# Gating two evictions behind until the fourteenth chunk, and other products in front of the third and fourth ffn_up steps

## What is computed

```
def conv_ffn(h, w_up, conv_w, conv_b, w_down, rows, cols):
    z = (h @ w_up).reshape(b, rows, cols, 2 * D_FF)
    z = lax.conv_general_dilated(z, conv_w[:, :, None, :], window_strides=(1, 1), padding='SAME', ...,
                                 feature_group_count=2 * D_FF)
    z = z.reshape(b, l, 2 * D_FF) + conv_b
    return (jax.nn.silu(z[..., :D_FF]) * z[..., D_FF:]) @ w_down
```

## Time and profile before

| | |
|---|---|
| median of 3 runs | 726.49 us (726.19 to 726.83) |
| profiled execution | 727.04 us in all, span 725.1 us |
| TensorE busy | 711.3 us (98%), mean granted clock 0.998 |
| VectorE, GpSimd, ScalarE busy | 497.7, 390.5, 364.4 us |
| chunks (ffn_up 1 to ffn_down 10) | 265.05 to about 447 us |

### The profile page before, as it was taken

One profiled execution on the slowest core, in us unless ns is written; L12 is line 12 of the kernel. 1 busy time (PEld: TensorE's weight loads), 2 busy tenths in 40 slices (PEclk: granted clock), 3 DMA queues, 4 the chain that ended last, 5 costly groups with the idle time before them and its releaser, 6 DMA issues.

```text
span 725.1 us, 14262 instructions
## 1 busy us (share of the span) xinstructions
PE 711.3 (98%) x5866; PEld 689.2 (95%) x5866; DVE 497.7 (69%) x919; ACT 364.4 (50%) x482; POOL 390.5 (54%) x225
## 2 busy tenths in 40 slices
PE   6899999999999999999999999999999999999998
PEld 3798889999999999999999999999999999999998
DVE  4886897569616569987777774557956666566563
ACT  6689235245434676555555556445563534334331
POOL 0767553547557958698888888766786000000000
PEclk9999999999999999999999999999999999999999
DMA  8994878336634565365555554433435655654511
GB/s 360 421 413 175 348 296 308 151 117 234 233 117 147 202 252 179 129 233 195 213 175 180 213 189 174 160 132 118 164 129 181 226 197 170 214 200 168 215 59 59
DMA packets 21234, 145.85 MB, mean 201 GB/s; under 512 B 2481, under 2 KB 3249, under 8 KB 3890
## 3 DMA queue, kind: packets, MB, share of 16 engines
q1 hardware_dynamic: 21024, 144.87, 55.1%
q10 hardware_dynamic: 146, 0.07, 0.0%
HBM read 143.88 MB, written 1.05 MB: 200 GB/s over the span
## 4 chain that ended last, share of the span: by engine, by line
PE 97%; DVE 1%; ACT 1%; issue 1%; DMA 0%; ACTq 0%; DVEq 0%
PE bank L1514 25%; PE bank L1516 25%; PE bank L1515 25%; PE bank L1533 5%; PE CP L1514 2%; PE CP L1516 2%; PE CP L1515 2%; PE bank L1630 2%; PE bank L1558 1%; PE CP L1547 1%; PE bank L1573 1%; PE bank L1919 1%; PE bank L1540 0%; PE bank L1742 0%; PE bank L1669 0%
## 5 line engine op out<-in xcount | busy, mean ns | idle before, releaser
L484 POOL TENSOR_TENSOR wlo<-raw,whi 128x512 fp32r<-128x512 f32 (+1 forms) x191 | 354.7, 1890 | 138.5 <-ACT whi L502 138.5
L502 ACT ACTIVATE whi<-raw 128x2048 fp32r<-128x2048 f32 x100 | 191.3, 1914 | 49.2 <-DMA raw<-in_w_in 26.8
L1281 DVE SCALAR_TENSOR_TENSOR Y<-bank,vec,Y 128x189 f32<-128x189 f32 (+2 forms) x344 | 120.8, 424 | 27.7 <-ACT Y L783 27.7
L1514 PE MATMUL bank<-H2h,whi 128*128 128x256 f32 x336 | 93.9, 279 | 2.0 <-DVE H2l L1248 1.3
L1515 PE MATMUL bank<-H2l,whi 128*128 128x256 f32 x336 | 93.2, 277 | 0.0
L1516 PE MATMUL bank<-H2h,wlo 128*128 128x256 f32 x336 | 93.2, 277 | 0.0
L1514 PE MATMUL bank<-H1h,whi 128*128 128x256 f32 (+1 forms) x288 | 89.8, 312 | 2.3 <-ACT H1h L568 2.0
L1515 PE MATMUL bank<-H1l,whi 128*128 128x256 f32 (+1 forms) x288 | 88.2, 306 | 0.0
L1516 PE MATMUL bank<-H1h,wlo 128*128 128x256 f32 (+1 forms) x288 | 88.2, 306 | 0.0
L916 DVE TENSOR_TENSOR wlo<-raw,whi 128x2048 fp32r<-128x2048 f32 x29 | 66.4, 2292 | 31.6 <-ACT whi L502 31.6
L1514 PE MATMUL bank<-H4h,whi 128*128 128x256 f32 x256 | 70.9, 277 | 0.0
(11 more groups left out here) (358 smaller groups left out, 1963.0 us busy)
## 6 DMA issues: line engine op xcount, KB each, us to landing
raw<-in_w_mlp SPq DMA_DIRECT2D x32, 1024.0 KB, 4.9
raw<-in_w_in SPq DMA_DIRECT2D x30, 1024.0 KB, 5.8
raw<-in_ffn_up SPq DMA_DIRECT2D x22, 1024.0 KB, 4.8
raw<-in_ada_hi SPq DMA_DIRECT2D x16, 1024.0 KB, 5.2
raw<-in_ffn_down SPq DMA_DIRECT2D x11, 1024.0 KB, 4.9
raw<-in_w_out SPq DMA_DIRECT2D x8, 1024.0 KB, 4.8
ada_s<-in_ada_s SPq DMA_DIRECT2D x4, 1024.0 KB, 17.9
ada_p<-in_ada_p SPq DMA_DIRECT2D x2, 1024.0 KB, 10.0
```

What stands on the lines that cost most here:

```text
L484: m = e.tensor_tensor(l[:, a:a + step], r[:, a:a + step], h[:, a:a + step].bitcast(F32), ALU.subtract)
L502: e.activation(whi[q % NHI][:, :], raw[n % NRAW][:, :], ACT.Copy).then_inc(s["w_hi"], 1)
L1281: e.scalar_tensor_tensor(o[:, r0:r1, c0:c1], z[:, r0 + dr:r1 + dr, c0 + dc:c1 + dc], cw[:, f, tap:tap + 1], o[:, r0:r1, c0:c1], ALU.mult, ...
L1514: e.matmul(out, h[:, col:col + P], xh, start=first, stop=False, skip_group_check=True)
```

## The change

ScalarE stays two evictions ahead of the gating up to chunk 14, and there gates two chunks, 12 and 13; from then on the order is the old one. On TensorE `settle` goes. Ahead of ffn_up 2 come 16 column products of SQ1 (8 tiles, two each), ahead of ffn_up 3 two row products, both into bank 7 and unused.

```
             chunk_out(i)
-            if 2 <= i <= 4:
+            if 2 <= i <= 14:
                 chunk_gate(i - 2)
-            if i == 4:
-                chunk_gate(3)
-            if i >= 5:
+            if i >= 14:
                 chunk_gate(i - 1)
...
             if i == 2:
-                settle((bank[7], bank[7]), SQ1[:, 0:4, :], SQ1[:, 4:8, :])
+                square_columns(bank[7], SQ1, 0, KT)
+            if i == 3:
+                rows(bank[7], [wide(0), wide(1)], None)
             if i < 22:
                 pair("ffn_up", i, H2h, H2l, ready=h2_ready if i == 1 else None)
```

More of the change, by code:

```diff
@@ L1824, in h2_ready @@
             e.wait_ge(s["h2_lo"], KT + 1 + k + 1)
[L1826 to L1830, removed]
         def contract(name, j, xh, xl, slots, hi_sem, lo_sem, per, last):
```

## The result

The changed kernel took 734.56 us (median of 4 runs, 731.13 to 738.02), the kernel before 726.51 beside it (4 runs, 726.19 to 726.83): ratio 1.0111, 95% interval 1.0063 to 1.0158. It is slower, by 8 us where 2.8 were forecast, and it spreads over 7 us where these four runs of the kernel before spread over 0.6.

A forecast was written before the change was run, and what follows sets the result against it. The prediction took TensorE, busy 98% of the span, as the bound. Its terms, 1.70 + 0.44 - 1.06 - 0.79 + 1.01 + 1.47 = +2.77 us, gave 729.3 us for the median (729.8 profiled), range 727.2 to 732.2.

The forecast's parts named there:

- Column products: Ahead of ffn_up 2: 16 column products take 3.40 us where the settling products took 1.70, so +1.70 us.
- Row products: Ahead of ffn_up 3: two row products cost 0.36 us plus 0.08 at the next matmul, +0.44 us.
- Pace: Behind the row products, 240 matmuls (ffn_up 3 to 6, ffn_down 0) run 4.4 ns faster each, -1.06 us.
- The old pause: At ffn_up 7: TensorE's present wait goes, as ScalarE starts that step's high part earlier, -0.79 us.
- list of signs: What a profile would show; for ffn_up 7, GpSimd beginning the low part some 4 us before TensorE asks.
- The wait for VectorE's taps: At ffn_up 7: TensorE waits for chunk 4's taps, behind chunk 3's late gating, +1.01 us (0.8 if slow).
- ffn_up 17: ScalarE's catching up at chunk 14 delays the weights of ffn_up 17; TensorE stalls +1.47 us (0.85 if slow).
- first part: The reading of the old profile: the matmul pace went from 117.8 to 113.3 ns at the pause before 307.76 us.
- slow stretch: Rival, chance 0.25: a pause or product group leaves the stream slow, up to ffn_up 17 at most; 730.1 to 731.9 us.
- clock falls: Rival, chance 0.04: the one-column products bring TensorE's clock down, costing 1 us or more; 730.3 us and up.

The follow-up runs named there:

- e3: The changed kernel, but ScalarE stays two evictions ahead to the last chunk and gates chunks 20 and 21 at the end; 742.73 us, ratio 1.0167.
- e11: The changed kernel with ScalarE's catching up at chunk 20 instead of 14; 739.81 us, ratio 1.0142.
- e12: As e11, and at chunk 5 the gating of chunk 3 comes ahead of the high part of ffn_down 1; 740.43 us, ratio 1.0151.
- e7: The changed kernel run once more, unaltered; 735.93 us, ratio 1.0100.
- e2: The kernel before with the change's TensorE products and the old order of ScalarE; 730.68 us, ratio 1.0037.
- e8: The changed kernel with 8 column products ahead of ffn_up 2 instead of 16; 730.09 us, ratio 1.0032.
- e1: The kernel before with the change's ScalarE order and the old TensorE stream; 730.34 us, ratio 1.0015.
- e16: As e9, but the two row products stand inside ffn_up 3 and not ahead of it; 725.54 us, ratio 0.9970.
- e6: The kernel before with only the high part of ffn_up 7 issued ahead of the gating of chunk 3, settling products kept; 731.34 us, ratio 1.0041.
- e9: As e6, settling products kept, plus two row products ahead of ffn_up 3, against the kernel before; 731.55 us, ratio 1.0023.
- e5: As e6, but without settling products and with two row products ahead of ffn_up 3; 729.81 us, ratio 1.0023.
- e15: As e6, but without settling products and with four row products inside ffn_up 5; 729.92 us, ratio 0.9974.

## Why the prediction was wrong

It gave 729.3 (727.2 to 732.2), slower at 0.82. The direction is right, the time is 5.3 us off, and the waits, at nearly their forecast size, are the smaller part of the loss. By its steps:

1. *Column products*, +1.70: 3.49 us in place of 1.70. Right. What the step left out is that they pull the clock down.
2. *Row products*, +0.44: 0.36. Right.
3. *Pace*, -1.06: **this is the step that failed.** The 240 matmuls took 28.36 us, as before. The step read one case, slow ahead and fast behind, as "rows leave the stream fast". In this profile they left it slow: it was fast ahead of them (30 intervals of 114.0 ns up to 281.82) and 117.8 ns behind. It was also fast ahead in three of the four other profiles with a clock fall (e3, e11, e12; not e7), and slow in both without one (e2, e8), where the step came out as forecast (27.3 us). The trace of the kernel before, too, had the case against the step: at 52.47 the same four records left a slow stream slow.
4. *The old pause*, -0.79: gone as such; GpSimd's low part of ffn_up 7 ended at 306.15, over 4 us before TensorE had done ffn_up 6. (The prediction's list of signs has this low part begin some 4 us ahead; its sum has it ready then.)
5. *The wait for VectorE's taps*, +1.01, or 0.8 behind a slow stream: 0.82 behind a slow one, 1.05 behind a fast one (e8). Right in both forms, place and releaser too.
6. *ffn_up 17*, +1.47: 1.46, behind GpSimd's low part. Right.

The sum also lacked two terms. Behind the wait at ffn_up 17, 510 matmuls ran slow, +2.3 us; the prediction let a pause leave a slow stream only at ffn_up 7, within a rival at 0.25, though its own first part had shown that a pause can change the pace. And the clock, which the sum put at nothing: a rival at 0.04, with the price "1 us or more". By the span's mean clock it fell in 9 of 11 runs, at 1.5 us in one profile (1.79+1.41 less the forecast 1.70) and 3.2 in another, and in 0 of 12 with half the products. "256 to 259 us holds 1.70 us of them at 1.00" was evidence for 1.70 us, and it was used for 3.4. The Trainium skill ("TensorE: Matmul & The Clock Gate", Part 1) has the clock released by recent activity. Here it fell behind 3.49 us of one-column products through which the profile shows TensorE busy, to intervals of some 213 ns, the lower level.

So the rivals "slow stretch" and "clock falls" came together, and in four of five profiles with a fall the first fed on the second, by the fast stream that it left ahead of the rows. The waits added 1.49 us net (0.03+1.46), 1.69 forecast. The miss of the profiled execution, 734.5 against 729.8, is pace (0.09 in place of -1.06, and the 2.3 us behind ffn_up 17) and clock (1.41). Without a clock fall the change has 731.1 and 731.7 us (2 runs), inside the forecast range.

**Open.** What the two paces are in the hardware, and why rows turn the pace in one place and not in another. What decides the pace behind a pause. Behind the settling products it was, in all five profiles that have them, the pace of the last ten matmuls of ffn_up 1 (slow in before, e1 and e16, fast in e6 and e9), so the question moves to ffn_up 1, which waits for its operand tiles. e6 was slow in 10 of 12 runs, and e9, which adds rows to it, should have been fast in as many and was not. And whether ScalarE's order by itself shifts the chances at ffn_up 7; the runs of e1 are too few for that.

## What to carry to other kernels

Where a profile shows one long stream of equal matmuls, divide stretches by their count before costing any wait: here 4% of pace over 1500 matmuls was worth 6.7 us, eight times the idle time that the edit was after. A wait, or a small group of other products, in such a stream is priced by what the stream does behind it, and one profile is one draw of that, so run the kernel ten times and look for clusters first. If column products are wanted, keep them short: half of them inside a step and two row products ahead of the next gave 725.1 us (0.7 us from lowest to highest) in 10 of 10 runs. And before a rule is read from one place of a trace, look at every place that has the same group.

## What the runs showed of the hardware

- Two paces for identical matmuls of 256 columns at a granted clock of 1.00: 113.3 and 117.8 ns, kept for up to 1518 matmuls and, in the chunks, changed only at an interruption, of which the shortest was 0.2 us (e5). The Trainium skill ("TensorE: Matmul & The Clock Gate", Back-to-back issue gap) gives one formula for the gap of a single matmul, by which 256 columns would be an estimated 109 ns; neither pace is that.
- Two row products (four records, 0.36 us) turned the pace in 12 of 12 profiles where they were put into the chunks, in either direction, and in 12 of 17 at 52 us.
- The last feed-forward has the two paces as well: 1486 intervals of 113.3 ns in 16 profiles and of 117.8 in e15, 6.6 us apart.
- With 32 records of one-column products (3.4 us) the span's mean clock is 0.995 or lower in 9 of 11 runs of the change and 6 of 10 of e2; with 16 records (1.7 us) it is 0.997 or more in 12 of 12. The profiles show the fall behind these products (window at 0.76) or already within (0.84 and 0.66 in e7).
- The stream that waits at ffn_up 17 is listed with the releaser "issue", though GpSimd's low part ends 0.10 us before it goes on.
